# Attention probabilities turned by VectorE by way of HBM, memory keys in 512-column half-units, and a reordered transfer queue, in a one-core hybrid encoder step

## The reference

```python
def memory_kv(mem, g, w_k, w_v):
    mn = rmsnorm(mem, g)
    k = (mn @ w_k).reshape(B, N_MEM, MEM_HEADS, MEM_HEAD_DIM)
    v = (mn @ w_v).reshape(B, N_MEM, MEM_HEADS, MEM_HEAD_DIM)
    return k, v
...
    qm = mq_raw.reshape(B, L, MEM_HEADS, MEM_HEAD_DIM)
    sc = jnp.einsum('blhd,bmhd->bhlm', qm, mem_k).astype(f32) * (MEM_HEAD_DIM ** -0.5)
    a = jax.nn.softmax(sc, axis=-1).astype(x.dtype)
    att = jnp.einsum('bhlm,bmhd->blhd', a, mem_v).reshape(B, L, MEM_WIDTH)
```

## Time and profile before

| | |
|---|---|
| median of 3 runs (lowest, highest) | 840.46 us (839.85, 841.02) |
| the profiled execution: its own time, its span | 841.19 us, 839.4 us |
| TensorE's granted clock over the span | 0.998 |
| PE busy (matmuls) | 823.4 us, 98% of the span |
| weight loads of PE | 732.3 us, 87% |
| DVE busy | 586.7 us, 70% |
| ACT busy | 469.1 us, 56% |
| POOL busy | 62.8 us, 7% |
| transfers | 191.83 MB, mean 229 GB/s; 18692 packets under 512 B |

### The profile page before, as it was taken

How to read it: one execution, slowest core, us unless ns; L and a number is a source line. 1 busy time by engine, 2 the same in 40 slices (tenths; PEclk the granted TensorE clock), 3 DMA queues, 4 the chain that set the end, 5 groups by cost and what they waited for, 6 DMA issues and landing times. The chain is left out here.

```text
span 839.4 us, 12162 instructions
## 1 busy us (share of the span) xinstructions
PE 823.4 (98%) x4744; PEld 732.3 (87%) x4744; DVE 586.7 (70%) x820; ACT 469.1 (56%) x622; POOL 62.8 (7%) x113
## 2 busy tenths in 40 slices
PE   7999999999999999999999999999999999999995
PEld 7979989988989998899999999878888888888884
DVE  5665487773445456695565456778989889889894
ACT  5645577754333324554333336656877768767773
POOL 1000100010000000000000000020004102210410
PEclk9999999999999999999999999999999999999999
DMA  8659855327534536345436467589999999999970
GB/s 269 208 142 291 221 142 132 118 81 220 165 126 126 176 115 199 126 151 163 152 110 216 151 201 256 209 264 409 389 357 351 358 397 381 352 373 366 382 279 18
DMA packets 111841, 191.83 MB, mean 229 GB/s; under 512 B 18692, under 2 KB 76960, under 8 KB 111648
## 3 DMA queue, kind: packets, MB, share of 16 engines
q1 hardware_dynamic: 109824, 185.91, 65.0%
q0 software_dynamic: 1152, 3.41, 1.1%
q10 hardware_dynamic: 800, 1.66, 0.6%
HBM read 181.70 MB, written 10.03 MB: 228 GB/s over the span
## 5 line engine op out<-in xcount | busy, mean ns | idle before, releaser
L1643 DVE TENSOR_TENSOR w_r<-arena,w_r 128x2048 fp32r<-128x2048 f32 x96 | 217.0, 2286 | 27.6 <-ACT w_r L1239 27.6
L1634 DVE TENSOR_TENSOR unit_r<-arena,unit_r 128x2048 fp32r<-128x2048 f32 x63 | 144.3, 2291 | 131.2 <-ACT unit_r L1228 131.1
L793 PE MATMUL pj<-xn_r,unit_r 128*128 128x320 f32 x1536 | 233.2, 311 | 0.8 <-issue 0.8
L793 PEld LDWEIGHTS pj<-xn_r,unit_r 128*128 128x128 f32 x1536 | 225.6, 188 | 4.7 <-issue 3.7
L1130 PE MATMUL pj<-w_r,xg 128*128 128x512 f32 x768 | 191.0, 398 | 0.5 <-DVE xg L1627 0.4
L1239 ACT ACTIVATE w_r<-arena 128x2048 fp32r<-128x2048 f32 x96 | 180.3, 1909 | 2.7 <-DMA arena<-in_w_exp_down 2.0
L1130 PEld LDWEIGHTS pj<-w_r,xg 128*128 128x128 f32 x768 | 141.8, 188 | 31.5 <-DVE xg L1627 0.8
L1228 ACT ACTIVATE unit_r<-arena 128x2048 fp32r<-128x2048 f32 x63 | 120.9, 1919 | 44.4 <-PE pj L793 23.6
L1159 PE MATMUL pj<-w_r,hidT 128*128 128x512 f32 x384 | 93.3, 392 | 0.6 <-ACT hidT L1490 0.6
L1159 PEld LDWEIGHTS pj<-w_r,hidT 128*128 128x128 f32 x384 | 71.8, 188 | 17.0 <-issue 0.8
L793 PE MATMUL pj<-br_r,unit_r 128*128 128x320 f32 x384 | 59.6, 311 | 0.0
(11 more groups left out here) (344 smaller groups left out, 793.3 us busy)
## 6 DMA issues: line engine op xcount, KB each, us to landing
arena<-in_w_in SPq DMA_DIRECT2D x40, 1024.0 KB, 5.5
arena<-in_w_exp_gate SPq DMA_DIRECT2D x64, 512.0 KB, 4.9
arena<-in_w_exp_up SPq DMA_DIRECT2D x64, 512.0 KB, 6.7
arena<-in_w_exp_down SPq DMA_DIRECT2D x64, 512.0 KB, 5.6
arena<-in_w_mem_v SPq DMA_DIRECT2D x4, 1024.0 KB, 5.3
arena<-in_w_br_mem SPq DMA_DIRECT2D x4, 1024.0 KB, 5.1
arena<-in_w_br_mlstm SPq DMA_DIRECT2D x4, 1024.0 KB, 5.1
arena<-in_w_br_gmlp SPq DMA_DIRECT2D x4, 1024.0 KB, 4.9
```

What stands on the lines that cost most here:

```text
L793: last = mm(bank_of(s)[0:out_rows, 0:out_cols], l, r, start=k == 0, stop=k == len(pairs) - 1)
L1634: v.tensor_tensor(unit_part(n, 1), raw_columns(n), unit_part(n, 0), ALU.subtract).then_inc(u_lo, 1)
L1643: v.tensor_tensor(w_r[u % NS][:, 1, :], raw_w[u % NS], w_r[u % NS][:, 0, :], ALU.subtract).then_inc(m_lo, 1)
```

## The change

1. The second half of `w_mem_k` (columns 512 to 1023) is projected in two half-units of 512 columns (`memk2`) in place of two 256-column units. The number of units stays.
2. The memory tokens lie in another order: partition p of tile t holds token 2p + t, for `mem_prompt`, the stored keys and values, and the cached values.
3. Step `pt` no longer uses TensorE or PSUM. SP stores the probabilities of head h to an HBM tensor `probabilities` (`store_probs`, two transfers) and reads them back in four transfers of 256-byte blocks (`load_probs`). VectorE turns them with one blockwise transpose of 128x640. One semaphore, `s_turned`, counts the turns of keys and probabilities.
4. The events stand elsewhere: `pt` h one or more pieces later, `av` h after pieces 6, 9, 12 and 14. Behind piece 6 also stands the turn of the keys of head 2, behind piece 8 the turn of head 1's probabilities (after the maxima of head 2), behind piece 9 the turn of the keys of head 3.
5. SP's order: the gate weights go behind unit 4; the gate rows are written ahead of unit 10 and read back behind it; keys are stored behind unit 11, maxima behind 12, values behind 14; stores and loads of probabilities stand behind units 16 to 21. Step `bc` comes two `mq` pieces later.

```diff
-    for u in range(4):
+    for u in range(2):
         n = unit("w_mem_k", u * 256)
...
+    wide("memk2", "w_mem_k", 0, 1, 2, "AA", lambda u, kh, i: early.pop(0)())
...
-            if c < H:
-                step("bc", c, ring=None, eng=None)
+            if 2 <= c < H + 2:
+                step("bc", c - 2, ring=None, eng=None)
...
-    pt = lambda h: (step("pt", h, 0), step("pt", h, 1))
+    pt = lambda h: step("pt", h, ring=None, eng=None)
-    events = [(ka, 0), (sc, 0), (ka, 1), (pt, 0), (sc, 1), (av, 0), (ka, 2), (pt, 1), (sc, 2), (av, 1), (ka, 3),
-              (pt, 2), (sc, 3), (av, 2), (pt, 3), (av, 3)]
+    events = {0: [(ka, 0)], 1: [(sc, 0)], 2: [(ka, 1)], 4: [(sc, 1)], 5: [(pt, 0)], 6: [(av, 0), (ka, 2)], 8: [(sc, 2), (pt, 1)],
+              9: [(av, 1), (ka, 3)], 10: [(sc, 3)], 11: [(pt, 2)], 12: [(av, 2)], 13: [(pt, 3)], 14: [(av, 3)]}
...
-                sp.dma_start(mem_tm[:, i, :], I["mem_prompt"][0, i * 128:(i + 1) * 128, :]).then_inc(s_mem[i], 16)
+                sp.dma_start(mem_tm[:, i, :], I["mem_prompt"][0].rearrange("(p t) d -> t p d", t=2)[i]).then_inc(s_mem[i], 16)
...
+            def store_probs(h):
+
+                sp.wait_ge(s_prob, 2 * h + 2)
+                sp.dma_start(p_store[h % 2, 0:TP].rearrange("(i p) m -> p i m", p=128), probs[:, h % 2, 0:2, :]).then_inc(s_written, 16)
+                sp.dma_start(p_store[h % 2, TP:T], probs[0:TS, h % 2, 2, :]).then_inc(s_written, 16)
+
+            def load_probs(h):
+
+                sp.wait_ge(s_written, 16 + 32 * (h + 1))
+                if h:
+                    sp.wait_ge(s_turned, TURNED["pt", h - 1])
+                for a in range(4):
+                    sp.dma_start(probs_b[32 * a:32 * a + 32, h % 2, 0:2 * T].rearrange("i (b d) -> i b d", d=64),
+                                 p_store[h % 2].rearrange("(b i) (a d) -> a i b d", i=32, d=64)[a]).then_inc(s_back, 16)
...
+                if n == 10:
+                    write_gate_rows()
                 if n >= 3:
                     sp.wait_ge(u_lo, n - 2 if n < 5 else n - 1)
...
-                if n == 6:
+                if n == 4:
+                    load_gate_weights()
+                elif n == 6:
...
                 elif n in (16, 18):
-                    sp.wait_ge(s_kmT, n - 14)
+                    sp.wait_ge(s_turned, TURNED["ka", n // 2 - 8, 1])
                     load_cached_keys(n // 2 - 6)
                     load_prompt_keys(n // 2 - 6)
-                elif n in (19, 21):
-                    sp.wait_ge(*done("av", (n - 19) // 2, 1))
-                    load_cache_v((n - 15) // 2)
+                    if n == 16:
+                        store_probs(0)
+                    else:
+                        load_probs(1)
+                elif n == 17:
+                    load_probs(0)
+                    store_probs(1)
+                elif n == 19:
+                    sp.wait_ge(*done("av", 0, 1))
+                    load_cache_v(2)
+                    store_probs(2)
+                elif n == 20:
+                    load_probs(2)
+                    sp.wait_ge(*done("av", 1, 1))
+                    load_cache_v(3)
+                    store_probs(3)
+                elif n == 21:
+                    load_probs(3)
...
-                elif kind == "pt":
-                    h, which = a
-                    pe.wait_ge(s_prob, 2 * h + which + 1)
-                    for j in range(2):
-                        for i in ((0, 1) if which == 0 else (2,)):
-                            n = TILES[i][1]
-                            c0 = j * 256 + i * 128 if which == 0 else j * 64
-                            last = tr(b[:, c0:c0 + n], probs[0:n, h % 2, i, j * 128:j * 128 + 128], ident[0:n, 0:n])
                 elif kind == "av":
                     h, which = a
-                    pe.wait_ge(*done("pt", h, which))
+                    pe.wait_ge(s_turned, TURNED["pt", h])
...
                 elif kind == "pt":
-                    h, which = a
+                    h, = a
                     if h >= 2:
-                        dve.wait_ge(*done("av", h - 2, which))
-                    t0, n = (0, TP) if which == 0 else (TP, TS)
-                    v.tensor_copy(pT[:, h % 2, :, t0:t0 + n], b[:, 0:2 * n].rearrange("p (a t) -> p a t", t=n)).then_inc(free, 1)
+                        dve.wait_ge(*done("av", h - 2, 1))
+                    dve.wait_ge(s_back, 16 + 64 * (h + 1))
+                    v.transpose(pT[:, h % 2, :, :].rearrange("p t (b i) -> p t b i", i=32), probs_b[:, h % 2, 0:2 * T].rearrange("p (b j t) -> p t b j", j=32, t=2)).then_inc(s_turned, 1)
```

More of the change, by code:

```diff
@@ L125, in make_steps @@
             step("qk", c, ring="pj", eng="A", unit=n, last=c % 2 == 1)
-            f, h = events.pop(0)
-            f(h)
+            for f, h in events.get(c, ()):
+                f(h)
             if c:
                 step("conv", c - 1, ring=None, eng=None)
-            if f is sc:
-                step("probs", h, 0, ring=None, eng=None)
-                step("probs", h, 1, ring=None, eng=None)
+            for f, h in events.get(c, ()):
+                if f is sc:
+                    step("probs", h, 0, ring=None, eng=None)
+                    step("probs", h, 1, ring=None, eng=None)
             if c % 2:
@@ L205 @@
 STEPS, UNITS = make_steps()
+TURNED = {(_s["kind"],) + _s["args"]: _k + 1 for _k, _s in enumerate(_s for _s in STEPS if _s["kind"] in ("ka", "pt"))}
 NBANK = {"pj": 4, "ms": 4, "hx": 3}
@@ L323, in build_kernel @@
         kmT = take(2, 2, 2, NMEM)
+        probs_b = at(off[0], 2, 3 * NMEM)
         probs = take(2, 3, NMEM)
@@ L440, in build_kernel @@
         v_store = nc.dram_tensor("v_rows", (128, 2 * H * (HD + 2)), FP32, kind="Internal").ap()
+        p_store = nc.dram_tensor("probabilities", (2, T, NMEM), FP32, kind="Internal").ap()
         x_rows = nc.dram_tensor("x_rows", (T, D), FP32, kind="Internal").ap()
@@ L644, in store_memory @@
                 sp.dma_start(O["mlstm_m_sample"][0, 0, :].rearrange("(h a) -> h a", a=1), rows[0:H, R_MM, T - 1:T]).then_inc(s_mout, 16)
+            def store_memory(name, src):
                 sp.wait_ge(*done("memv", 1, 1, 1))
[L646 to L648 removed]
+                for i in range(2):
+                    sp.dma_start(O[name][0, 0].rearrange("(p t) h d -> t p (h d)", t=2)[i], src[:, i, :]).then_inc(s_memout, 16)
             def store_conv():
@@ L956, in _ @@
                     pe.wait_ge(*done("mq", 2 * h + 1))
-                    pe.wait_ge(s_kmT, 2 * h + which + 1)
+                    pe.wait_ge(s_turned, TURNED["ka", h, which])
                     for q, i in enumerate((0, 1) if which == 0 else (2,)):
@@ L1325, in _ @@
                     if h >= 2:
-                        act.wait_ge(*done("pt", h - 2, which))
+                        act.wait_ge(s_turned, TURNED["pt", h - 2])
                     for q, i in enumerate((0, 1) if which == 0 else (2,)):
@@ L1732, in _ @@
                     if h == 0:
[L1733 removed]
+                        dve.wait_ge(s_back, 16)
                     r = rbb[:, h, :]
@@ L1753, in _ @@
                     src = memk_b[:, h, :] if which == 0 else cmk[:, h % 2, :]
-                    v.transpose(kmT[:, h % 2, which, :, :].rearrange("p t (b i) -> p t b i", i=32), src.rearrange("p (b j t) -> p t b j", j=32, t=2)).then_inc(s_kmT, 1)
+                    v.transpose(kmT[:, h % 2, which, :, :].rearrange("p t (b i) -> p t b i", i=32), src.rearrange("p (b j t) -> p t b j", j=32, t=2)).then_inc(s_turned, 1)
                 elif kind == "sc":
```

36 lines of the change are left out of this document (18 added, 18 removed).

## The result

The changed kernel is slower: 846.72 us median of 6 runs (845.53 to 849.58), against 840.25 (839.85 to 841.02, 6 runs) for the kernel before. Ratio 1.0078, 95% interval 1.0068 to 1.0088, so 5.7 to 7.4 us. The forecast was 843.1, with a range of 839.4 to 846.6: the side is right, the size is not, and the median lies just outside the range.

What follows compares the result with a forecast made beforehand. The prediction took TensorE, busy nearly throughout, to bound the kernel. Its terms -0.6 - 1.0 - 0.8 - 3.2 + 8.2 gave +2.6, added to 840.46 for 843.1 us, range 839.4 to 846.6.

Steps and rivals of the forecast that it cites:

- Keys in 512 columns: Key projection on TensorE: 48 matmuls of 512 columns replace 96 of 256, 12.0 us become 11.4, -0.6 us.
- the gate weights: Issued behind unit 4, they let unit 3 load sooner; TensorE's 1.04 us gap at 31.25 goes, -1.0 us.
- `bc`: Two pieces later, its exponential no longer delays unit 10's rounding on ScalarE; TensorE's 0.82 us gap at 82.42 goes, -0.8 us.
- The transposes: Step `pt` leaves TensorE, 0.80 us per head for four heads, -3.2 us.
- The new path: Probabilities through HBM land 7.7 us after the unit load's issue; TensorE waits at heads 0 to 3, +8.2 us.
- The clock falls: Rival: granted clock halves after each of three TensorE waits, 2.8 us a gap, 8.4 in all, 851.5 us; chance 0.02.
- eat up the gains: Rival: with a delay of 6.7 us the three large waits shrink by 1.0 each, -0.4 in all, 840.1 us; chance 0.27.
- reads that come back in time: Rival: probabilities land within 5.1 us, before the unit ahead of them, 834.9 us; chance 0.10 with the half-way case.
- Reads at half the key blocks' rate: Rival: probability reads are slower, delay 9.7 us, every head waits 2.0 longer, +8, 851 us; chance 0.08.
- Front gains that fail: Rival: unit 3 still lands late or the gates step waits for weights, losing 1.0 to 2 us, 844 to 845; chance 0.08.

Runs made afterwards that it cites:

- the last experiment: The changed kernel with 1.95 us of idle identity matmuls on TensorE ahead of `av` 2 alone, waits before `av` 0 and `av` 3 left bare: 846.03 us, ratio 1.0067.

## Why the prediction failed

The waits were there and of the size that the sum gave them. The step that failed is the clock: the sum puts its fall at nothing, and among the rivals it has 0.02; the runs show that it falls after part of the waits and costs 2.3 of the 3.9 us that are missing. The other 1.6 go by terms that the runs only partly resolve.

*Keys in 512 columns, -0.6, the gate weights, -1.0, and `bc`, -0.8.* Together the median moved by 1.7 in place of 2.4, with an interval (1.0 to 2.5) that still holds 2.4. For the keys the traces settle what the medians can't. From unit 2's first matmul to the row that stands at 46.49 in the earlier trace rows it takes 21.03 us with 256-column units and the gate weights late (24.20 to 45.23), and 20.46 in the changed kernel (25.15 to 45.61), both without a gap: 0.57 less, as priced. `bc` gave at least its price. If a term was oversized it is the gate weights': the gap of 1.04 belongs to one execution, which took 841.19 us where the median is 840.25, and another one has 0.52 there. The prediction took that gap out of a slow execution, subtracted the 0.7 by which this execution was slow, and kept the gap whole. That this is where the 0.7 went is likely and not shown.

*The transposes, -3.2.* Right, by the stretch from the first scores to `v` in the version with the reads ahead. The 9.4 us that the Trainium skill's figure (VectorE: DVE Perf Modes, The three transpose paths) came to, as an estimate, did not show: 3.2 did.

*The new path.* The delay from the load's issue to the landing was put at 7.7; the turn began 7.4 to 8.2 after that issue. The waits were predicted as 2.4, 0.3, 2.6 and 2.9, in all 8.2. With the clock kept up they were 3.07, 0.36, 2.72 and 2.25, in all 8.4. That the sum comes out so well is partly luck: head 0 waited 0.7 longer than predicted and head 3 0.65 shorter. The turn takes 0.84, as predicted. Head 1 was in time, as predicted, and VectorE's convolution and split behind the turn made no gap ahead of a piece. In the execution of the changed kernel shown above `av` 3 waits only 1.26, since TensorE came there late: the time that the slow `av` 2 lost is taken off that wait. (Point 4 of the change calls every `pt` h later; `pt` 2 stands behind the same piece as before and `pt` 3 one piece sooner. The working for heads 2 and 3 used the right places.)

*The sum, then.* The profiled execution with all waits filled took 844.06 us, 2.9 above the profiled execution of before; the sum said +2.6. By medians the same kernel is 4.4 above before (844.44 against 840.04). So of the 3.9 us between the forecast's +2.6 and the +6.5 measured, 2.3 are the clock. Of the other 1.6, 0.7 is what the front gave less than its 2.4 by the medians, and 0.2 the longer waits; the rest I can't assign to a term. The sum's gaps were read in an execution that lies 1.15 above that 840.04, and no run shows that a gain read there carries over whole to the median.

*"The clock falls", 0.02.* This is the step that failed. The prediction said that "the rows show the clock at 1.00 through a gap of 1.04 us only" and gave the rival 0.02. But the row is no reason against it: from its first 14 us (1.58 and 1.27 us of idleness there) to its last matmul the trace of before has no longer gap, so there it is silent about gaps of two or three microseconds. Its end does say something. TensorE's last matmul of before ends at 830.78, and the windows behind it (columns as in rows 1) show the clock at its upper level for some five microseconds of idleness and then at the lower one:

```profile
834.00:836.00 2.00, 0.00 (x0) 0.00 (x0) 0.17 (x1) 0.14 (x1) 0.98 (x1) 1.00 0.03 8
836.00:838.00 2.00, 0.00 (x0) 0.00 (x0) 0.00 (x0) 0.00 (x0) 0.00 (x0) 0.50 0.42 156
```

So the trace of before did show that idleness brings the clock down, though not that two or three microseconds of it can. The Trainium skill (TensorE: Matmul & The Clock Gate, HAM oscillation) describes a kernel in which each wait for a transfer drops the clock. Here the runs agree that such waits can do it, but not that each does: 3.12 us ahead of `av` 0 in the changed kernel left the clock at 1.00, while 2.63 and, in the last experiment, 3.48 and 2.15 did not. The price was off as well. The prediction had 2.8 a gap and 8.4 for three. A fall costs 1.6, since it ends 3.1 to 3.5 us after TensorE starts again, and what it delays comes off the next wait where one follows; the three waits together cost 2.3 in the median, between the changed kernel and the one with fillers. On top of the forecast 2.3 make 845.4.

*The range.* Its low end rested on shorter delays that no row showed, and its high end on the delay alone; nothing in it stood for the clock. The working comes to 847.1 for the high end, and 846.6 was given without a reason. With 847.1 the median of 846.72 would have lain inside, but by luck: the delay was not 8.7, and the waits of 8.4 with the clock kept up end at 844.44.

*The other rivals.* With a delay of 7.4 to 8.2, not 6.7, the waits did more than eat up the gains. For reads that come back in time the prediction asks for a delay of at most 5.1, "7.7 less the smallest large wait"; that difference is 5.3, and for all three waits to go it would have to be 7.7 less the largest, 4.8. The rival came true only by another order of the queue. It would have given 834.9 by the prediction, 5.6 below 840.46; that order gave 836.11, 3.9 below its own 840.04. Of the 1.7 between 5.6 and 3.9, 0.7 is the front's and 0.6 the waits of 0.15 and 0.46 that were left; 0.4 stays open. Reads at half the key blocks' rate: no, the delay was not 9.7. Front gains that fail: no, both gaps are gone.

**What stays open.** Which executions lose the clock at which wait. The length of the gap does not decide it by itself, as the waits above show, and the mean clock of a run is too coarse to count the falls, since it also counts the low clock behind the last matmul, which costs nothing: 841.47 us with 0.994 and 841.54 with 0.998 are both executions of the kernel before. Whether the new order of tokens costs some tenths at the start was not settled.

## What to carry to other kernels

A small transfer that an engine waits for must not stand behind a large one in its queue: here the place of four 80 KB reads, ahead of a 1 MB load or behind it, was worth 10.6 us with the clock falls that the waits brought, more than three times the 3.2 that the change had taken off TensorE. When a change makes TensorE wait where it never did, price the wait and, besides, the slow stretch after it, even if the trace of before shows nothing of the kind: a trace is silent on gaps longer than those it has, and its idle end is a place to see whether the clock falls at all. And where gains are read as gaps out of one execution, compare that execution with the median before subtracting from the median.

## What was unexpected of the hardware

The granted clock went from 1.00 to 0.50 after TensorE had been idle for 2.15, 2.63 and 3.48 us, and stayed at 1.00 through 3.12 us in another place, with dense matmuls before each; behind the last matmul of before it stayed at 1.00 for some five microseconds. Each fall ended within 4 us of work and cost 1.6 us. Idle matmuls of 1.95 us, which left 1.12 us of idleness at most, kept the clock up in the profiled execution and made the kernel 2.3 us faster in the median, with its five runs within 1.1 us, though they compute nothing. And the 256-byte reads of a tensor that had just been written landed a median 2.3 us after their issue when no load stood ahead of them, against 5.3 behind the load of a unit or the key blocks.
